# GpSimd in place of VectorE for the division of the probabilities in causal attention over head pairs

## The reference

```python
def causal_attention(q, k, v):
    ...
    def one_block(args):
        q_blk, blk = args
        sc = jnp.einsum('bqhd,bkhd->bhqk', q_blk, k,
                        preferred_element_type=jnp.float32) * scale
        q_pos = blk * Q_BLOCK + jnp.arange(Q_BLOCK)
        mask = k_pos[None, :] <= q_pos[:, None]
        sc = jnp.where(mask[None, None], sc, -jnp.inf)
        p = jax.nn.softmax(sc, axis=-1).astype(v.dtype)
        return jnp.einsum('bhqk,bkhd->bqhd', p, v)
...
        tok = causal_attention(q, k, v).reshape(b, s, TOK_WIDTH)
        mem_out = memory_attention(q_mem..., mem_kv[:, :, 0], mem_kv[:, :, 1])
        y = jnp.concatenate([tok, mem_out], axis=-1) * jax.nn.silu(gate)
        h = layer_norm(ALPHA * h + y @ w_out[layer], ln_g[layer], ln_b[layer])
```

## Time and profile before

| | |
|---|---|
| median of 3 runs | 3577.27 us (3573.75 to 3585.76) |
| span of the profiled execution | 3578.9 us |
| the attention of `rest` within it | 2722 to 3024 us |
| of it the six latent pairs | about 2771 to 3002 us, 38 us each |
| PE busy, whole span | 3274.2 us (91%) |
| DVE busy, whole span | 1949.7 us (54%) |
| POOL busy, whole span | 1561.2 us (44%) |

### The profile page before, as it was taken

The page is one execution under the profiler, slowest core; times in us unless marked ns, Lnnn a source line. Parts: engine busy times, 40 slices in busy tenths (PEclk is TensorE's granted clock), DMA queues, the critical chain, the costliest instruction groups (busy, mean ns, idle before and its releaser), DMA issues. The chain is left out here.

```text
span 3578.9 us, 45809 instructions
## 1 busy us (share of the span) xinstructions
PE 3274.2 (91%) x17652; PEld 2587.5 (72%) x17652; DVE 1949.7 (54%) x2824; ACT 1156.5 (32%) x2265; POOL 1561.2 (44%) x1195
## 2 busy tenths in 40 slices
PE   5888999999699999889999999999897999899796
PEld 2666787788598888667788878887674566676465
DVE  3278854545444455587733373338413887665736
ACT  4144432333333333332211021102223664144713
POOL 1114645455143441156666666666551001554332
PEclk9988869999899999899999999999996999999887
DMA  4335536232253442343333333334434321222112
GB/s 166 89 106 165 154 118 185 86 83 83 69 140 98 122 125 65 105 144 94 89 94 100 95 89 100 94 100 104 141 101 119 79 60 50 83 81 59 47 52 72
DMA packets 524317, 358.55 MB, mean 100 GB/s; under 512 B 92497, under 2 KB 477382, under 8 KB 524102
## 3 DMA queue, kind: packets, MB, share of 16 engines
q1 hardware_dynamic: 513446, 325.22, 31.6%
q0 software_dynamic: 4608, 16.78, 1.5%
q10 hardware_dynamic: 6048, 13.63, 1.1%
HBM read 276.85 MB, written 78.18 MB: 99 GB/s over the span
## 5 line engine op out<-in xcount | busy, mean ns | idle before, releaser
L2403 PE MATMUL psum<-place,place 128*128 128x512 f32 x2126 | 862.7, 406 | 80.5 <-POOL place L2381 33.5
L2404 PE MATMUL psum<-place,place 128*128 128x512 f32 x2126 | 843.1, 397 | 0.0
L2405 PE MATMUL psum<-place,place 128*128 128x512 f32 x2126 | 841.0, 396 | 0.0
L2379 POOL CAST place<-place 128x1024 fp32r<-128x1024 f32 (+3 forms) x302 | 304.7, 1009 | 1119.9 <-PE psum L2405 674.8
L2381 POOL TENSOR_TENSOR place<-place,place 128x1024 fp32r<-128x1024 f32 (+3 forms) x302 | 691.3, 2289 | 24.2
L2403 PEld LDWEIGHTS psum<-place,place 128*128 128x128 f32 x2126 | 408.7, 192 | 197.9 <-POOL place L2381 51.8
L2404 PEld LDWEIGHTS psum<-place,place 128*128 128x128 f32 x2126 | 408.9, 192 | 90.3 <-issue 7.5
L2405 PEld LDWEIGHTS psum<-place,place 128*128 128x128 f32 x2126 | 408.3, 192 | 87.6
L659 PE MATMUL psum<-place,place 128*128 128x512 f32 (+1 forms) x712 | 289.0, 406 | 22.1 <-issue 10.5
L660 PE MATMUL psum<-place,place 128*128 128x512 f32 (+1 forms) x712 | 273.7, 384 | 0.0
L661 PE MATMUL psum<-place,place 128*128 128x512 f32 (+1 forms) x712 | 273.5, 384 | 0.0
(11 more groups left out here) (325 smaller groups left out, 5592.1 us busy)
## 6 DMA issues: line engine op xcount, KB each, us to landing
place<-in_w_mlp_up SPq DMA_DIRECT2D x64, 512.0 KB, 4.0
place<-in_w_mlp_down SPq DMA_DIRECT2D x64, 512.0 KB, 3.9
place<-in_w_out SPq DMA_DIRECT2D x48, 512.0 KB, 4.0
chunked<-place SPq DMA_DIRECT2D x64, 320.0 KB, 3.6
place<-in_w_in SPq DMA_DIRECT2D x34, 512.0 KB, 5.8
solve<-in_w_ada POOLq DMA_DIRECT2D x32, 512.0 KB, 6.2
place<-in_lru_w_in SPq DMA_DIRECT2D x32, 512.0 KB, 3.8
place<-in_mla_w_in SPq DMA_DIRECT2D x30, 512.0 KB, 4.2
```

What stands on the lines that cost most here:

```text
L2379: nc.gpsimd.tensor_copy(hi, raw).then_inc(self.w_split, 1)
L2403: pe.matmul(ps, self.w_hi[:, j, k, :], hi, start=(k == 0), stop=False)
L2404: pe.matmul(ps, self.w_hi[:, j, k, :], lo, start=False, stop=False)
L2405: mm = pe.matmul(ps, self.w_lo[:, j, k, :], hi, start=False, stop=(k == kt - 1))
```

## The change

For the six latent pairs the multiply of `divide` leaves DVE's stream and becomes an instruction of POOL's, in the new generator `gpsimd`. DVE still takes the reciprocal and signals `rden`; POOL waits for that, multiplies in place, and signals a new semaphore `shares`; PE's `turn` waits for `shares` in a latent pair and for `probs` in a memory pair. The two memory pairs keep their multiply on DVE, and so does `Recall`. All of `Attend`'s POOL instructions stand ahead of those of `Chain` in POOL's stream.

```diff
     DEPTH = PV = 2
+    SHARED = True
...
+        self.given = [sum(self.pooled(x) for x in range(g)) for g in range(self.G + 1)]
...
+    def pooled(self, g):
+
+        return self.SHARED and self.pairs[self.units[g // 2][0]]["causal"]
...
         def turn(g):
-            pe.wait_ge(self.probs, g + 1)
+            if self.pooled(g):
+                pe.wait_ge(self.shares, self.given[g] + 1)
+            else:
+                pe.wait_ge(self.probs, g - self.given[g] + 1)
...
             nc.vector.reciprocal(rd, tot).then_inc(self.rden, 1)
-            dve.wait_ge(self.rden, g + 1)
-            ts(p, p, rd, None, ALU.mult).then_inc(self.probs, 1)
+            if not self.pooled(g):
+                dve.wait_ge(self.rden, g + 1)
+                ts(p, p, rd, None, ALU.mult).then_inc(self.probs, 1)
...
+    def gpsimd(self, pool):
+        for g in range(self.G):
+            if self.pooled(g):
+                p = self.prob[:, g % 2, 0:self.blocks(g // 2) * P]
+                pool.wait_ge(self.rden, g + 1)
+                self.C.nc.gpsimd.tensor_scalar(p, p, self.st[g % 2][:, 3:4], None, ALU.mult).then_inc(self.shares, 1)
+                yield
...
# Recall:
     DEPTH = PV = 1
+    SHARED = False
...
# rest():
         @block.gpsimd
         def _(pool):
+            for _ in a.gpsimd(pool):
+                pass
             alternate(only(LIN, HELD), chain.gpsimd(pool), None, None, None, None, lru.clear(pool))
```

More of the change, by code:

```diff
@@ L1577, in begin @@
             self.first.append(self.first[-1] + -(-self.blocks(g // 2) // 4))
-        (self.fixed, self.scored, self.masked, self.maxed, self.negged, self.exped, self.rden, self.probs, self.turned,
-         self.copied, self.pv, self.evac, self.hi_done, self.lo_done) = (C.sem(f"{mark}_" + n) for n in (
-             "fixed", "scored", "masked", "maxed", "negged", "exped", "rden", "probs", "turned", "copied", "pv",
+        (self.fixed, self.scored, self.masked, self.maxed, self.negged, self.exped, self.rden, self.probs, self.shares,
+         self.turned, self.copied, self.pv, self.evac, self.hi_done, self.lo_done) = (C.sem(f"{mark}_" + n) for n in (
+             "fixed", "scored", "masked", "maxed", "negged", "exped", "rden", "probs", "shares", "turned", "copied", "pv",
              "evac", "hi_done", "lo_done"))
+        self.given = [sum(self.pooled(x) for x in range(g)) for g in range(self.G + 1)]
         self.loaded, self.sent = C.pair(f"{mark}_loaded"), [0, 0]
```

## The result

The changed kernel takes 3616.36 us (median of 4 runs, 3610.93 to 3624.1) against 3576.05 for the kernel before: a recorded ratio of 1.0119, 95% interval 1.0077 to 1.0161 (the two medians alone give 1.0113). It is 40 us slower; 3580.3 was predicted, with a range up to 3600.

The account below looks back on a forecast made before the run. PE nearly set the pace (35.62 of 38.0 us a latent pair), DVE close behind. Lateness +2, splits moved -1.8 and +2, L1728 +1 gave +3 us on the 3577.3 us median: 3580.3 us, range 3569 to 3600.

Parts of the forecast that it names:

- the lateness term of the sum: Latent pairs: transposes delayed by the slower multiply, less their room; about 0.35 us a pair, 2 us in six.
- Price of the multiply on POOL: Multiply in latent pairs: priced between CAST and two-input instruction, 0.47 us at 256 columns, 1.27 at 1024.
- The first rival: Latent-pair multiplies on POOL cost 1.91 us at 1024 columns; 3.25 us lost a pair, 3598 us in all; chance 0.21.
- the signs of being wrong: Closing list: prediction fails if POOL's price leaves its bounds, POOL stretches other DVE instructions, or PE's granted clock falls.
- my own table: Latent pairs, by tile size: 0.09 us plus POOL's time less DVE's, set against room, 0.5 us at 1024 columns.
- the second ceiling: Latent pairs: four multiplies on the chain of waits, 1.56 us a pair, could give back at most 9.4 us.
- VectorE's freed time is worth little: Latent pairs: some 8 us a pair freed on DVE mostly turns idle, since PE has only 2.4 us of gaps.
- a CAST-priced link would be hidden: Latent pairs: at the CAST's own price the 1024 case is hidden, 384 recovers nearly whole; about +0.5 us in all.
- The hand-over: Reciprocal to POOL to transposes: 0.09 us more on the way in, nothing more on the way out.
- VectorE was the bound and comes free: Latent pairs: four chain multiplies come back whole, 9.4 us, plus 1.8 of the sixth pair: -11 us, 3566 us; chance 0.05.
- The splits: Weight-tile splitting moves from the sixth latent pair, giving back 1.8 us, into the last memory pair, costing 2 us.
- L1728 against GpSimd: Latent pairs: DVE's instruction with two SBUF inputs, 12 times, sometimes blocked by POOL's multiply; 1 us in all, range 0 to 6.

Follow-up runs that it names:

- the CAST kernel: Changed kernel with GpSimd rounding the tile in place of the multiply, division left out: pairs of 38.07 us, ratio 1.0007 to the kernel before.
- the TENSOR_TENSOR kernel: Changed kernel with GpSimd multiplying by a broadcast column as TENSOR_TENSOR instead of TENSOR_SCALAR: pairs of 39.73 us, ratio 1.0031 to the kernel before.
- the rounding: Kernel before with the results' rounding to high and low parts moved from ScalarE and VectorE to GpSimd: pairs of 37.35 us, ratio 1.0006 twice.
- kernel with the multiply beside: Kernel before, VectorE keeping its multiply, plus a GpSimd TENSOR_SCALAR of the same shape on a spare tile: pairs of 38.03 us, ratio 1.0037.
- control: The kernel before, run once more unchanged: pairs of 38.02 us, attention 282.1 us, ratio 1.0005.

## Why the prediction was wrong

*The step that failed* is the one that the lateness term of the sum rests on, "Price of the multiply on POOL". It held the instruction to lie between the CAST and the TENSOR_TENSOR of the earlier trace rows and took a fifth of the way, 1.27 us for 1024 columns. It lies above both: 2.84 us for 1024, 1.24 for 384, 0.92 for 256 columns, that is about 0.28 us and 2.5 ns a column ((2843 - 603) / 896). I ordered the prices by the number of tensors that stream, and no row showed that order for arithmetic with a scalar. An operation that no row shows is not bounded by its neighbours. The first rival, "costs like a two-input instruction", had the mechanism and the side; even its price, 3598 us, was too low for the same reason.

*A second step failed with it.* The sum has no term for TensorE's clock; it stood only among the signs of being wrong, and that sign came true. The falls to 0.50 within the latent pairs cost about 8 us of the 45. They followed the long waits at 1024 columns, which the prediction didn't have since it priced them at 0.1 us. In the one profile of the kernel with only those multiplies on GpSimd the waits are there and the falls are not, so the waits don't bring them each time.

*The working behind it stands in the main.* With the measured prices my own table gives: 1024 columns 0.09 + 2.84 - 0.75 - 0.5 = 1.7 us; 896, 768, 640 and 512 columns (2.52, 2.20, 1.88, 1.56 us less VectorE's 0.68, 0.62, 0.55, 0.49) 1.4, 1.2, 0.9, 0.7; 384 columns 0.9; 256 columns 0.4: together 7.2 us a pair, 43 us in six. At the full clock 6.5 us a pair and 39 us were measured. That is closer than its terms deserve, and by luck. The 1024 tile alone costs 2.96 us and not 1.7, since GpSimd is still busy with the first head when the second is due. And the room of the tiles from 640 to 896 columns, which I had set to 0.5 without a row, is larger, as the trace of the kernel before had it:

```profile
2866.26 0.62 DVE L1711 TENSOR_SCALAR place<-place,cols 128x768 f32<-128x768 f32 x1
...
2867.97 0.87 PE L1648 MATMUL psum<-mats,place 128*128 128x128 f32 x6
...
2872.47 0.69 DVE L1711 TENSOR_SCALAR place<-place,cols 128x896 f32<-128x896 f32 x1
...
2874.53 0.98 PE L1648 MATMUL psum<-mats,place 128*128 128x128 f32 x7
```

From the end of the multiply to its transposes these are 1.1 and 1.4 us; at 640 columns the rows give 0.7 to 0.9, at 512 0.2 to 0.5. With these rooms I estimate about 2 us a pair from the table at two-input prices, where 3.25 stood in the prediction and 1.7 were measured, and 5.6 + 1.3 (GpSimd busy with the first head) = 6.9 at the measured prices. The two errors have opposite signs.

*A reading that was off.* The prediction has the transposes wait for L1711 "6 times out of 16", 2.8 us. Those six are entries of PE and PEld together; PE itself waited twice in the pair, 0.5 us. So the second ceiling, 9.4 us, was too high, and the run without any multiply gave back 0.10 us a pair.

*Point by point.* That VectorE's freed time is worth little was right: with no multiply anywhere a pair gains 0.10 us. That a CAST-priced link would be hidden (+0.5 us in all) was right: 38.07 us a pair, 0.05 x 6 = 0.3 us. The hand-over was right in size: reciprocal to GpSimd 2939.02 to 2939.12. The rival "VectorE was the bound and comes free" is out. *The splits:* charged 2 us for the last memory pair and -1.8 for the sixth. They came at 3037.19 to 3044.12, when GpSimd had done its last multiply, and met one multiply of VectorE's that was stretched to 0.68 us; the last pair took 21.6 us against 21.5. The 2 us were not there. In the CAST kernel they came at 3002.0 to 3009.0 and stretched two multiplies of the last memory pair to 2.13 and 0.88 us; it took 21.6 us as well. In the TENSOR_TENSOR kernel, where two were stretched to about 1.0 and 1.4 us, it took 22.1 us in one execution and 32.4 in the other, with the clock down (last section). The 1.8 given back can't be seen in a sixth pair of 47.3 us. *L1728 against GpSimd* (now L1738): charged 1 us, found 0.

```profile
2927.70 2.20 POOL L1761 TENSOR_SCALAR place<-place,cols 128x768 f32<-128x768 f32 x1 [0.42 <-DVE cols L1718]
...
2929.51 0.69 DVE L1738 TENSOR_TENSOR place<-place,place 128x512 fp32r<-128x512 f32 x1 [1.72 <-ACT place L1791]
```

It begins 0.39 us before GpSimd's end and keeps its 0.69 us, as all of them do.

## What to carry to other kernels

Before moving an instruction into a link that another engine waits for, get a row of that very operation on the new engine: the price of a relative is no bound. Ask of a moved instruction how much room its waiter has at each size, and read each room from its own rows, not how busy the engine is that it leaves; here 7.7 us a pair taken off VectorE was worth 0.1 us. Count a wait of TensorE by its matmuls alone, without the weight loads. When a change makes TensorE wait long, look whether its granted clock stays up: here that was about a sixth of the loss. If GpSimd has idle time, give it work that ends off the chain (the rounding, -0.67 us a pair, though too little to show in the whole time) rather than a piece of the link.

## What the runs showed of the hardware

GpSimd's TENSOR_SCALAR in float32 is dearer than its TENSOR_TENSOR: 2.84 and 1.91 us for 128x1024 by the same column, 2.77 with a constant, while a plain copy takes 1.04.

GpSimd and VectorE side by side were milder than the earlier trace rows suggest. Against TENSOR_SCALAR on GpSimd, VectorE's multiply of 1024 columns kept 0.75 us in 11 of 12 cases and GpSimd's gave way (3.41 us); a VectorE multiply of 128 columns was held to 1.04 us, but not until GpSimd's end; a VectorE instruction with two SBUF inputs (L1738) was not held in any of the seven cases in which the two overlapped. In the kernel before, a VectorE multiply beside a GpSimd TENSOR_TENSOR took 2.12 us, to just behind the latter's end. The Trainium skill, SBUF — State Buffer, section Who interferes with whom, has the one that issues second fully blocked when VectorE uses both its port pairs; the TENSOR_SCALAR rows don't agree with that, those of the earlier trace rows do.

TensorE's granted clock is not the same in each execution of one kernel. The last memory pair, 21.5 us at 1.00 before, took 32.4 us in one execution of the TENSOR_TENSOR kernel, in which PE had waited 0.53 us for a held VectorE multiply shortly ahead of the fall:

```profile
3004.00:3010.00 6.00, 4.95 (x33) 2.74 (x30) 4.42 (x13) 3.31 (x11) 3.42 (x3) 0.98 0.47 134
3010.00:3016.00 6.00, 6.00 (x25) 3.06 (x25) 3.60 (x16) 2.24 (x8) 0.00 (x0) 0.50 0.14 41
```

At 0.50, the 1.2 GHz level, that stretch costs 11 us; in the second execution of the same kernel the pair took 22.1 us. The kernel with the multiply beside had the same (33.3 us), about 2 us behind a wait of PE of 0.65 us for a VectorE multiply. The first latent pair was 37.4 us at 1.00 or 40.9 us at a mean of 0.89, in the same kernel (control and first profile). Each attention begins at 0.50; once the clock had risen, it fell within the latent pairs in no profile but the changed kernel's (five times). What tips it was not found. Together with the attention's start, which lay between 2709 and 2743 us over the fourteen profiles, this is why stages were compared here and not whole times.
